# Modulation products of a two-block transformer kernel: full-width products, or four column groups with a summing product, spread between the projections

## The reference

```
c_act = jax.nn.silu(c)
for l in range(DEPTH):
    mod = (c_act @ w_mod[l] + b_mod[l])[:, None, :]
    sh1, sc1, g1, sh2, sc2, g2 = jnp.split(mod, N_MOD, axis=-1)
    h = modulate(x, sh1, sc1)          # rms_norm(x) * (1 + scale) + shift
    mix = hybrid_mixer(h, ...)         # attention and a gated LRU in both directions, merged
    x = x + g1 * mix
    h = modulate(x, sh2, sc2)
    ff = swiglu(h, ...) if l % 2 == 0 else moe_swiglu(h, ...)
    x = x + g2 * ff
```

## Time and profile before

| | us |
|---|---|
| median of three timed runs | 3220.65 |
| lowest and highest of them | 3213.65, 3225.9 |
| the profiled execution's own time | 3222.14 |
| its span in the trace | 3220.4 |

### The profile page before, as it was taken

One profiled execution on the slowest core, in us unless ns is written; L12 is line 12 of the kernel. 1 busy time (PEld: TensorE's weight loads), 2 busy tenths in 40 slices (PEclk: granted clock), 3 DMA queues, 4 the chain that ended last, 5 costly groups with the idle time before them and its releaser, 6 DMA issues. The chain is left out here.

```text
span 3220.4 us, 35304 instructions
## 1 busy us (share of the span) xinstructions
PE 3044.9 (95%) x13934; PEld 2333.8 (72%) x13935; DVE 1714.8 (53%) x1892; ACT 1415.2 (44%) x1665; POOL 19.0 (1%) x43
## 2 busy tenths in 40 slices
PE   7999989899997999999999999997999899999898
PEld 4665769868475877878778778775746797756697
DVE  1135135412435888987988889872521553341354
ACT  1233034311404777776777777652311443231343
POOL 0000000000000000000000000001000000000000
PEclk9999989999998999999999999998999999999999
DMA  7355434544734999999999999956322353413252
GB/s 283 133 186 196 176 129 165 180 150 173 249 106 173 367 327 333 366 332 365 332 327 369 331 325 369 331 203 205 131 78 79 140 200 121 159 62 131 85 197 78
DMA packets 310609, 695.69 MB, mean 216 GB/s; under 512 B 6246, under 2 KB 25172, under 8 KB 310500
## 3 DMA queue, kind: packets, MB, share of 16 engines
q1 hardware_dynamic: 308096, 689.07, 59.3%
q0 software_dynamic: 1792, 4.90, 0.5%
q10 hardware_dynamic: 612, 0.18, 0.0%
HBM read 693.07 MB, written 1.05 MB: 216 GB/s over the span
## 5 line engine op out<-in xcount | busy, mean ns | idle before, releaser
L1904 DVE TENSOR_TENSOR ring_rest<-ring,weights_hi 128x2048 fp32r<-128x2048 f32 x270 | 605.2, 2286 | 34.2 <-ACT weights_hi L1500 33.3
L1500 ACT ACTIVATE weights_hi<-ring 128x2048 fp32r<-128x2048 f32 x270 | 514.4, 1920 | 125.2 <-PE ps L1282 78.9
L977 PE MATMUL ps<-arena,ring 128*128 128x256 f32 x2368 | 527.4, 385 | 4.8 <-ACT arena L1500 4.3
L977 PEld LDWEIGHTS ps<-arena,ring 128*128 128x128 f32 x2368 | 454.7, 193 | 76.5 <-issue 6.6
L1500 ACT ACTIVATE arena<-ps 128x512 f32<-128x512 f32 (+7 forms) x279 | 148.7, 542 | 637.1 <-PE ps L977 293.1
L1280 PE MATMUL ps<-weights_hi,xg_hi 128*128 128x512 f32 x1008 | 403.2, 400 | 3.5 <-DVE xg_lo L1904 3.5
L1282 PE MATMUL ps<-weights_hi,xg_lo 128*128 128x512 f32 x1008 | 395.9, 393 | 0.0
L1500 ACT ACTIVATE arena<-arena 128x256 f32<-128x256 f32 (+5 forms) x240 | 135.0, 594 | 455.2 <-DVEq L1960 190.4
L1281 PE MATMUL ps<-ring_rest,xg_hi 128*128 128x512 f32 x792 | 310.7, 392 | 0.0
L1299 PE MATMUL ps<-weights_hi,hidden_split_moe 128*128 128x512 f32 x1008 | 281.9, 391 | 0.0
L1904 DVE TENSOR_TENSOR late_rest<-arena,weights_hi 128x2048 fp32r<-128x2048 f32 x108 | 244.7, 2287 | 6.1 <-ACT weights_hi L1500 4.3
(11 more groups left out here) (173 smaller groups left out, 3354.4 us busy)
## 6 DMA issues: line engine op xcount, KB each, us to landing
ring<-in_moe_w_gate_dram SPq DMA_DIRECT2D x54, 2048.0 KB, 7.9
ring<-in_moe_w_up_dram SPq DMA_DIRECT2D x45, 2048.0 KB, 7.8
ring<-in_moe_w_down_dram SPq DMA_DIRECT2D x36, 2048.0 KB, 7.8
ring<-in_mlp_w_dram SPq DMA_DIRECT2D x32, 2048.0 KB, 8.7
arena<-in_moe_w_down_dram SPq DMA_DIRECT2D x27, 2048.0 KB, 8.0
ring<-in_w_in_dram SPq DMA_DIRECT2D x26, 2048.0 KB, 9.2
ring<-in_w_mod_dram SPq DMA_DIRECT2D x24, 2048.0 KB, 7.9
arena<-in_moe_w_up_dram SPq DMA_DIRECT2D x18, 2048.0 KB, 7.9
```

Source lines behind the costliest of these rows:

```text
L977: mm = pe.matmul(o, w[:, k, c:c + P], act[:, k, :], start=(k == 0), stop=(k == ks - 1))
L1500: return act.activation(o, i, func, **kw)
L1904: return dve.tensor_tensor(o, a, b, op)
```

## The change

Each 512-column piece of the modulation is now computed in four column groups: product k = 4r + j (r = 0, 1; j = 0 to 3) takes 32 copies of a column of `c_act` as the stationary operand and writes to partitions 32j to 32j + 31, so each group sums two of the eight k, and all 32 partitions of a group hold the same row. The four group rows then have to be added. For shift and scale that is done while turning: the stationary operand is 128 columns of the copied 128 x 512 tile, the moving one a column of 1/32. For the gates a full product with a 128 x 128 tile of 1/32 sums the groups and puts the result on all partitions, and a product of one partition (a row of ones by the bias row) adds the bias. ScalarE then copies the result to `gb` or `modc`.

The pieces are spread: one behind each of the projections qkv, gx, sg, ya and yl, and the summing product of a piece stands behind the products of the next one. Vectors 3, 4, 2, 5 come between qkv and sg; vectors 0 and 1 of layer 1 begin behind the last sg projection of layer 0 and go on between ya and yl. Nothing is left of the blocks of modulation work between sg, the backward gates, attention and ya. `Tiles` and `Stream` get the same order. The first four pieces stay at the start, and VectorE copies 128 rows of them in place of one; the 16 turning products stay too. VectorE's four additions to `gb` go, and the bias is loaded as one row. `mod_ready` of layer 1's first pair moves behind layer 0's wo branch.

```diff
+def later_mods(l):
+    of = [(l, v) for v in (3, 4, 2, 5)] + [(1, v) for v in (0, 1) if l == 0]
+    return [(layer, v, c) for layer, v in of for c in range(2)]
...
-                    load(gb[:, i], wide(I["b_mod"][l, v * D:(v + 1) * D]), "gates_landed")
+                    load(gb[0:1, i], I["b_mod"][l:l + 1, v * D:(v + 1) * D], "gates_landed")
...
-                        for k in range(KD):
-                            mm = pe.matmul(b[0:1, :], cact[:, k:k + 1], w[:, k, :],
-                                           start=(k == 0), stop=(k == KD - 1))
-                        done(mm)
+            def mod_rows(l, v, c):
+                w = wcols(("mod", l, v, c), 512)
+                b = open_bank(("mr", l, v, c))
+                for r in range(2):
+                    for j in range(4):
+                        k = 4 * r + j
+                        mm = pe.matmul(b[32 * j:32 * j + 32, :], cact[:, k:k + 1].to_broadcast([P, 32]), w[:, k, :],
+                                       start=(r == 0), stop=(r == 1))
                 done(mm)
+
+            def mod_columns(b, rows, n):
+                for i in range(n):
+                    mm = pe.matmul(b[:, i:i + 1], rows[:, i * P:(i + 1) * P], part_sum[:, 0:1],
+                                   start=True, stop=True)
+                return mm
+
+            def modulation(l, i):
+                chunks = later_mods(l)
+                if i < len(chunks):
+                    mod_rows(*chunks[i])
+                if 1 <= i <= len(chunks):
+                    layer, v, c = chunks[i - 1]
+                    wait_emptied(pe, ("mr", layer, v, c))
+                    b = open_bank(("mf", layer, v, c))
+                    if v in (2, 5):
+                        pe.wait_ge(sem("gates_landed"), 32 * (l + 1))
+                        pe.matmul(b, part_sum, row_part, start=True, stop=False)
+                        done(pe.matmul(b, ones_row, gb[0:1, v // 3, c * 512:(c + 1) * 512], start=False, stop=True))
+                    else:
+                        done(mod_columns(b, row_part, 4))
...
                 for c in range(4):
                     project_T("sg", l, ("sg", l, c), hT, 2, 2 * c)
-
-                mod_rows("mB", l, (3, 4))
+                    modulation(l, 5 + c)
+
                 lru_gates(1)
-                mod_columns("mB", l)
...
-                            mm = pe.matmul(acc(i, c), cact[:, k:k + 1].to_broadcast([P, P]), w[:, k, :],
-                                           start=(k == 0), stop=(k == KD - 1))
...
-                if l == 0:
-                    mod_rows("mA", 1, (0, 1))
-                    mod_columns("mA", 1)
...
+            def modulation(l, i):
+                chunks = later_mods(l)
+                if i < len(chunks):
+                    b = full(act, ("mr", *chunks[i]))
+                    if i:
+                        act.wait_ge(pe_done, value[("mf", *chunks[i - 1])])
+                    elif l:
+                        act.wait_ge(pe_done, value[("mf", *later_mods(0)[-1])])
+                    empty(f(row_part, b, ACT.Copy), ("mr", *chunks[i]))
+                if 1 <= i <= len(chunks):
+                    layer, v, c = key = chunks[i - 1]
+                    b = full(act, ("mf", *key))
+                    if v in (2, 5):
+                        empty(f(gb[:, v // 3, c * 512:(c + 1) * 512], b, ACT.Copy), ("mf", *key))
+                    else:
+                        at = {0: 0, 1: KD, 3: 2 * KD, 4: 3 * KD}[v] + 4 * c
+                        empty(f(modc[:, layer, at:at + 4], b[:, 0:4], ACT.Copy), ("mf", *key))
...
-                for i in range(4):
-                    o = full(act, ("mB_row", l, i))
-                    empty(f(mod_row[0:1, i], o[0:1], ACT.Copy), ("mB_row", l, i))
                 lru_gates(1)
...
+                wait_emptied(dve, ("mf", l, 5, 1))
                 add_branch(("wo", l), gb[:, 0], tmp1)
```

More of the change, by code:

```diff
@@ L156, in __init__ @@
         self.add(("c",), "act")
-        self.rows("mA", 0, "dve")
+        for v, c in FIRST_MODS:
+            self.add(("mr", 0, v, c), "dve")
         for i in range(5):
@@ L183, in __init__ @@
             self.attention([("gqa", h) for h in range(HEADS)], l, 1)
-            if l == 0:
-                self.rows("mA", 1, "dve")
-                self.add(("mA", 1), "dve")
-            for j in range(4):
-                self.add(("ya", l, j), "dve")
-            for j in range(4):
-                self.add(("yl", l, j), "dve")
+            for c in range(2):
+                for j in range(2):
+                    self.add(("ya", l, 2 * c + j), "dve")
+                self.modulation(l, 9 + c)
+            for c in range(2):
+                for j in range(2):
+                    self.add(("yl", l, 2 * c + j), "dve")
+                self.modulation(l, 11 + c)
             for t in range(TT):
@@ L237, in __init__, with modulation @@
             self.hidden("mlp", (l,), FF2 // P // 2)
-    def rows(self, name, l, who):
-        for c in range(4):
-            self.add((name + "_row", l, c), who)
+    def modulation(self, l, i):
+        chunks = later_mods(l)
+        if i < len(chunks):
+            self.add(("mr", *chunks[i]), "act")
+        if 1 <= i <= len(chunks):
+            self.add(("mf", *chunks[i - 1]), "act")
     def hidden(self, name, at, n):
@@ L374, in __init__, with mod @@
         self.at = {key: n for n, key in enumerate(self.items)}
-    def mod(self, l, which, step):
-        for i, v in enumerate(which):
-            for c in range(2):
-                self.add(("mod", l, v, c), (step, l, 2 * i + c))
+    def mod(self, l, i):
+        chunks = later_mods(l)
+        if i < len(chunks):
+            self.add(("mod", *chunks[i]), ("mr", *chunks[i]))
     def add(self, key, last_read):
@@ L498, in program @@
         probsT1 = [pp[:, 3 + i, :] for i in range(2)]
+        part_sum = one.cut(P)
+        ones_row = Region(one.pos, P).cut(P)[0:1]
+        one.cut(P)
+        row_part = one.cut(512)
         rope_tmp = Region(pp_at, 2560).cut(3, 10 * 2 * 32)
@@ L1025, in mod_columns @@
-            def mod_columns(name, l):
-                wait_emptied(pe, (name + "_row", l, 3))
-                b = open_bank((name, l))
-                for i in range(2 * KD):
-                    mm = pe.matmul(b[:, i:i + 1], mod_row[0:1, i // 4, (i % 4) * P:(i % 4 + 1) * P],
-                                   ident[0:1, 0:1], start=True, stop=True)
-                done(mm)
+            def mod_rows(l, v, c):
[6 more added lines that the diff above has]
+                                       start=(r == 0), stop=(r == 1))
+                done(mm)
@@ L1666, in _ @@
                 attention([("gqa", h) for h in range(HEADS)], 1, l, HD ** -0.5)
+                for i in range(9, 13):
+                    modulation(l, i)
                 deviation(x, xn, "x_ready", 2 * l + 1, True)
@@ L2052, in _ @@
             normed(x, xn, "xn_ready")
-            for i in range(4):
-                o = full(dve, ("mA_row", 0, i))
-                empty(dve.tensor_copy(mod_row[0:1, i], o[0:1]), ("mA_row", 0, i))
+            for i, (v, c) in enumerate(FIRST_MODS):
+                o = full(dve, ("mr", 0, v, c))
+                empty(dve.tensor_copy(mod_row[:, i], o), ("mr", 0, v, c))
             for i, dst in enumerate((vt1[:, 0], vt1[:, 1], bmT[:, 0], bmT[:, 1], vt2)):
```

107 lines of the change are left out of this document (54 added, 53 removed).

## The result

| | before | after |
|---|---|---|
| median, 20 executions each, us | 3217.36 | 3222.85 |
| lowest and highest | 3213.1, 3225.9 | 3219.17, 3231.17 |
| profiled execution, own time | 3222.14 | 3228.36 |
| span | 3220.4 | 3226.2 |

The ratio is 1.0019, 95% interval [1.0012, 1.0027]: the medians lie 5.5 us apart, inside the 0.5% that I called no change. The predicted time was 3227, by a sum of +5.6 us. The size came out. But the profile will show that the sum over the part that I worked out is +0.6 and not +5.6, and that 5.2 us come from a part of the program in which nothing was changed. Both profiled executions are slower than their kernel's median, by 4.8 and 5.5 us.

What follows compares the result with a forecast made beforehand. TensorE was taken as full, covering a ScalarE and VectorE chain that would end the stretch behind sg. Layer 0 -1.8, layer 1 +20.4, start -13.0: together +5.6 us, forecast 3227, range 3211 to 3268.

Steps and rivals of the forecast that it cites:

- What bounds the stretch: From sg to the query/key transposes, 65.9 us of TensorE work cover about 61.6 us of a ScalarE and VectorE chain.
- rival 3: Whole kernel: TensorE's sum is the time, the LRU chain does not end the stretch; 3122 us, chance 0.03.
- Chunk, 1.9 us: One 512-column modulation piece in four column groups running side by side takes 1.9 us, where it took 6.9.
- rivals 1 and 2: Column groups: 1, no overlap, 6.9 us a chunk, 3337, chance 0.15; 2, partial overlap, 3.6 a chunk, 3259, chance 0.14.
- Between the projections, 24.1: Before the end of sg, eight chunks with their folds add 24.1 us per layer to TensorE's path.
- From sg to the copies, -4.2 and -6.7: From the end of sg to VectorE's copies of the transposes, 4.2 us gained in layer 0 and 6.7 in layer 1.
- Attention, +3: Attention, entered at 1.2 GHz after TensorE's idle stretch, costs 3 us more per layer, bounds 0 and 6.
- The start, -13.0: First four chunks, each waiting for its DMA: transposes start at 34.3 instead of 47.26 us, gain 13.0, bounds 11 and 15.
- Layer 1's pair, -24.7: Layer 1's shift and scale, after layer 0's attention: moving and cheapening these products gains 24.7 us.
- The part behind: From layer 1's second transposes to the end, where nothing was changed: forecast 0.

Runs made afterwards that it cites:

- e3: The kernel before, with one of eight products per chunk in modulation vectors 3, 4, 2 and 5 of both layers: 3072.89 us, ratio 0.9544.
- e4: The kernel before, with only the start and layer 1's first pair (vectors 0 and 1) as in the changed kernel: 3182.99 us, ratio 0.9883.
- e6: e4 with the rows of vectors 3 and 4 computed in column groups, in their old place: 3171.57 us, ratio 0.9845.
- e1: The changed kernel with each chunk as eight full-width products, no column groups, summed with 1/128: 3326.02 us, ratio 1.0331.
- e5: The changed kernel with added products that nobody reads, where TensorE idles under the LRU chain: 3215.63 us, ratio 0.9987.
- e11: The changed kernel with two added products that nobody reads, between layer 1's two yl projections: 3221.61 us, ratio 1.0004.

## Why the prediction came out, step by step

- **What bounds the stretch.** Right. The chain of ScalarE and VectorE ends it: in e3, with 7/8 of the products gone, 54.4 us are left of 66.9; rival 3 (TensorE's sum, 3122) is out by e3 and e4, and by e6, where 40 us less work gave 11.4 between the medians.
- **Chunk, 1.9 us.** 1.85 in the profile, 3.59 with two groups, 6.87 with one; rivals 1 and 2 are out. The row groups of the differential scores were the right model. As for the Trainium skill's 2.38x for three column tiles ("TensorE: Matmul & The Clock Gate", Part 3: Packing small matmuls), by which I had estimated 2.2 us: here four groups gave 3.71x, and the measurement decides. The drain at a change of tiling mode of which the skill speaks ("TensorEngine Tiling (Array Packing)", Key Properties) is small here: from one chunk to the next, without the chunk itself, TensorE takes 16.12 us with four groups (232.15 - 216.03) and 15.92 in e1 without groups (279.75 - 263.83), so both changes of mode together cost 0.2 us. The 0.1 us per border that the prediction read from the earlier trace rows fits.
- **Between the projections, 24.1.** Mis-sized: 26.2 in layer 1. The gate fold was 2.11 and not 1.73, because each of its matmuls takes 0.53 and not 0.433 (three folds, +1.1); the projections between chunks take 14.01 (232.15 - 218.14) where two took 27.6, so 0.2 more for each of seven, which was not in the sum (+1.4); the chunks were 0.05 cheaper (-0.4). In layer 0 the same cost shows as 24.1 because TensorE was at full clock from 44.5 on, before only from 63.5: 4.4 us of projections at 1.2 GHz less, half of which, 2.2, came back.
- **From sg to the copies, -4.2 and -6.7.** Mis-sized: -6.7 and -8.1. I had 4.3 late, 7.0 won in the middle, 2.8 for the gates' second half at 1.2 GHz. The middle was worth 8.3, since the table load, too, moved ahead of the wait (251.39, the scan ends at 258.42). ScalarE's decay began 5.2 after sg, 4.5 later than before. The half cost 1.3, 0.85 of it a wait ahead of the last six sigmoids. 4.5 - 8.3 + 1.3 = -2.5, where the forecast had +0.1.
- **Attention, +3.** Mis-sized: +1.2 in layer 1; the most in any profile is 25.9 us in place of 24.0, so 1.9. The forecast's 3 was a guess between 0 and 6.
- **The start, -13.0.** Right, -13.3, and -12.75 at the transposes by which it was forecast (47.26 to 34.51). As forecast, the fourth chunk ran at 1.2 GHz (3.46 us). Its working had 30.4 + 3.5 = 33.9 and wrote 34.3, with no reason for the 0.4; the chunk began at 31.13. In six profiles with this same start the first transposes of layer 0 stand at 40.5 to 42.6, so the last digit means little.
- **Layer 1's pair, -24.7.** Right: with attention +1.9, layer 0 loses 22.5 from the copies to the second transposes, so the pair alone -24.4.
- **The part behind.** The step that failed is the one that I did not write: I costed it at nothing. It cost +5.2 in the profiled execution, 4.5 of it in two stretches with the same matmuls at a lower granted clock. The terms that I did write are 5.0 too high together, so the total met by an error on each side. The mechanism of the middle (a chain that ends the stretch, projections under which nothing hides) is shown by experiments; that the profiled total, +6.2, fits the +5.6 within 0.6 us is luck. The medians differed by 5.5 and, in the repeat, by 2.6.

## What to carry to other kernels

Cheaper products are a gain only where TensorE is what ends the stretch; under a chain of other engines they are free up to its length, and the best place for long ones is there, cut so that a piece fills each hole (3160.4 us with 15 us more TensorE work than the changed kernel). Take small pieces out of exposed places and leave the rest under cover: half of this change is worth 36 us and the whole of it nothing. Busy time does not tell: TensorE's fell by 87.6 us here, and the time of the kernel did not. And a difference of some 5 us between two profiled executions of 3200 can come from where the low stretches of the clock fall in untouched code: cut both profiles at the same marks before a cause is named, and look where the profiled execution lies among the timed ones.

## What the runs showed of the hardware

- Two matmuls in each of 2 rounds by four column groups of 32, 512 columns in float32: 1.85 us for 16; two groups 3.59, one 6.87. At full clock the four matmuls of a round start within 0.02 us. Going from full products to column groups and back cost 0.2 us together.
- A product of one partition by 512 columns is no cheaper than one of 128: 0.53 a matmul (L1068 beside L1067, 1.05 us each for two); behind full-width chunks (e1) 1.05 beside 0.95. Full matmuls take 0.433 each where 42 stand in a row (18.19 us in e5).
- The granted clock fell in stretches where TensorE idled or ran short pieces, and at 294.9 (e5) also 4.2 us after the end of 24.2 us of full products at clock 1.00. With 1.73 us of products added far ahead (e11), and the part beginning 3.2 us later, the low stretch at the router was 6.8 and 17.1 us in place of 27.3; the changed kernel repeated its low stretches in another session, and the kernel before all but one.
